# Weights stored by column tiles, squares of x by columns, a conv unit in spare banks and late gate parts by quadrant, in a one-layer hybrid decoder step

## The reference

```python
q, k, v, h, B, C = split(rms_norm(x) @ w_in)            # 6 x 1024 columns
a = dilated_attention(q_normed, k_normed, v)            # 16 heads of 64
c = B * short_conv(C * h)
h1 = x + concat[rms_norm(a), rms_norm(c)] @ w_out
h2 = h1 + (silu(n @ w_gate) * (n @ w_up)) @ w_down      # n = rms_norm(h1), D_FF 5632
y = h2 + sigmoid(rms_norm(h2) @ w_ple_gate) * (p @ w_ple_proj)
```

## Time and profile before

| | |
|---|---|
| median of 3 runs | 2556.58 us (2554.0 to 2557.53) |
| the profiled execution's own time | 2558.73 us |
| its span, first to last instruction | 2557.2 us |
| TensorE busy | 2487.2 us (97%), 20452 matmuls |
| VectorE, ScalarE, GpSimd busy | 1744.7 (68%), 934.6 (37%), 254.2 (10%) us |
| mean granted TensorE clock | 0.989 of 2.4 GHz (its other level is 0.5, 1.2 GHz) |
| DMA | 328.26 MB, 128 GB/s in the mean |

### The profile page before, as it was taken

One profiled execution on the slowest core, in us unless ns is written; L12 is line 12 of the kernel. 1 busy time (PEld: TensorE's weight loads), 2 busy tenths in 40 slices (PEclk: granted clock), 3 DMA queues, 4 the chain that ended last, 5 costly groups with the idle time before them and its releaser, 6 DMA issues.

```text
span 2557.2 us, 51857 instructions
## 1 busy us (share of the span) xinstructions
PE 2487.2 (97%) x20452; PEld 2470.9 (97%) x20452; DVE 1744.7 (68%) x2185; ACT 934.6 (37%) x1202; POOL 254.2 (10%) x285
## 2 busy tenths in 40 slices
PE   5999999999999989999999999999999999999998
PEld 5999999999989979999999999999899999999998
DVE  3576877787786879888888898898533322356433
ACT  4232333333332444444444444444332211233331
POOL 1111110111021000000000000000000000143000
PEclk8999999999999989999999999999999999999999
DMA  7444343434334434544444454444665543233342
GB/s 230 134 127 121 107 123 95 120 109 126 107 110 135 133 91 117 152 127 133 132 115 136 127 148 131 116 132 117 207 212 171 164 145 121 83 92 99 110 116 66
DMA packets 477677, 328.26 MB, mean 128 GB/s; under 512 B 18330, under 2 KB 452762, under 8 KB 476584
## 3 DMA queue, kind: packets, MB, share of 16 engines
q1 hardware_dynamic: 449488, 250.25, 34.6%
q0 software_dynamic: 27248, 74.89, 8.9%
q10 hardware_dynamic: 880, 2.31, 0.3%
HBM read 291.06 MB, written 40.65 MB: 130 GB/s over the span
## 4 chain that ended last, share of the span: by engine, by line
PE 89%; DMA 4%; DVE 4%; issue 1%; ACT 1%; POOL 0%; DVEq 0%; SPq 0%; ACTq 0%
PE acc L538 17%; PE acc L542 17%; PE acc L540 16%; PE acc L731 11%; PE acc L730 11%; PE acc L732 11%; DMA wraw<-in_w_in 3%; DMA wraw<-in_w_down 1%; DVE wlo L1172 1%; PE aux L549 1%; PE aux L581 1%; ACT whi L845 0%; PE aux L625 0%; DVE slots_c L1180 0%; PE aux L554 0%
## 5 line engine op out<-in xcount | busy, mean ns | idle before, releaser
L1172 DVE TENSOR_TENSOR wlo<-wraw,whi 128x1024 fp32r<-128x1024 f32 (+1 forms) x276 | 333.1, 1207 | 421.2 <-ACT whi L845 420.5
L845 ACT ACTIVATE whi<-wraw 128x1024 fp32r<-128x1024 f32 (+1 forms) x276 | 285.3, 1034 | 729.8 <-PE acc L542 616.5
L730 PE MATMUL acc<-xb_hi,whi 128*128 128x260 f32 x1232 | 349.4, 284 | 11.9 <-DVE xb_lo L1553 11.9
L731 PE MATMUL acc<-xb_lo,whi 128*128 128x260 f32 x1232 | 349.6, 284 | 0.0
L732 PE MATMUL acc<-xb_hi,wlo 128*128 128x260 f32 x1232 | 349.1, 283 | 0.0
L730 PE MATMUL acc<-xa_hi,whi 128*128 128x260 f32 x1232 | 348.8, 283 | 0.0
L732 PE MATMUL acc<-xa_hi,wlo 128*128 128x260 f32 x1232 | 348.8, 283 | 0.0
L731 PE MATMUL acc<-xa_lo,whi 128*128 128x260 f32 x1232 | 348.7, 283 | 0.0
L538 PE MATMUL acc<-slots_a,whi 128*128 128x260 f32 x1536 | 314.9, 287 | 0.0
L542 PE MATMUL acc<-slots_a,wlo 128*128 128x260 f32 x1536 | 310.2, 284 | 0.0
L540 PE MATMUL acc<-slots_a,whi 128*128 128x260 f32 x1536 | 308.3, 282 | 0.0
(11 more groups left out here) (266 smaller groups left out, 4980.4 us busy)
## 6 DMA issues: line engine op xcount, KB each, us to landing
wraw<-in_w_in SPq DMA_DIRECT2D x96, 512.0 KB, 4.0
blocks<-in_w_gate SPq DMA_DIRECT2D x88, 512.0 KB, 6.3
blocks<-in_w_up SPq DMA_DIRECT2D x88, 512.0 KB, 6.1
wraw<-in_w_down SPq DMA_DIRECT2D x48, 448.0 KB, 3.7
wraw<-in_w_out SPq DMA_DIRECT2D x32, 512.0 KB, 3.9
wraw<-in_w_ple_gate SPq DMA_DIRECT2D x32, 512.0 KB, 3.9
slots_b<-f_dram SPq DMA_DIRECT2D x28, 520.0 KB, 4.7
f_dram<-sig_t POOLq DMA_DIRECT2D x22, 520.0 KB, 3.2
```

The source lines that it names most:

```text
L730: mm(to, w_h, hi[:, n, X_OF[u], :], start=p == 0, stop=False)
L731: mm(to, w_h, lo[:, n, X_OF[u], :], start=False, stop=False)
L845: on(whi[:, u % HILO, 0:width], wraw[:, u % RAW, 0:width], ACT.Copy).then_inc(s_whi, 1)
L1172: V.tensor_tensor(wlo[:, u % HILO, 0:width], wraw[:, u % RAW, 0:width], whi[:, u % HILO, 0:width].bitcast(F32), ALU.subtract).then_inc(s_w ...
```

## The change

- **Weights by column tiles.** On the host every weight matrix is laid out as [column tile, 128 partitions, k tiles x 128], so that a unit is one run of 4 KB for each partition where it was eight of 512 B. Which bytes are loaded when is the same. The gate and up blocks keep even and odd k tiles apart.
- **The start.** The first weight goes ahead of x on SP's queue, and x's first load moves to ACT's. The second copy of x by rows is gone, with POOL's four loads and its wait for them; the keys' load follows the skew and row-bias stores at once. ScalarE squares the 16 column tiles (5, 5 and 6 of them behind the splits of weights 4, 5 and 6), VectorE adds them up, and TensorE sums the result by columns behind unit 2. The root and the reciprocal come in the same places of the lists as before.
- **The conv half.** The root goes ahead of ScalarE's split of weight 4, and the queries' upper halves one step later. VectorE's reciprocal comes first; its split of weight 4 and `norm_q` follow the first output tile. The transposes go to the scores' bank, and unit 2 to the two spare banks of the attention, so it waits for neither accumulator.
- **The gate's start.** The parts' upper and lower halves are made by kind (all even tops, all odd halves, then the sums). The sums of pair 6 get buffers of their own, and are added beside the attention half; the fourth sum has its sign turned when it is added, with negated gains. TensorE begins with the first four units on the early parts (the third in spare banks), then finishes unit 0 on the even tops, most of unit 2 on the odd ones, and units 1 and 3 as the sums come. The last square and the norm's sum come behind unit 4.

```diff
+X_SQUARES = (range(0, 5), range(5, 10), range(10, KT))
...
-            sp.dma_start(wraw[:, u % RAW, 0:nk * width].rearrange("p (k m) -> p k m", k=nk),
-                         w[k0 * P:(k0 + nk) * P, bass.ds(col, width)].rearrange("(k p) m -> p k m", p=P)
-                         ).then_inc(landed[u % RAW], 16)
+            sp.dma_start(wraw[:, u % RAW, 0:nk * width],
+                         w[bass.ds(tile, 1), :, k0 * width:(k0 + nk) * width].squeeze(0)).then_inc(landed[u % RAW], 16)
...
                 if first and n == 0:
-                    load_x(2)
-                load(at, 2 * n + 1, w_in, KU, KU, j * P + kind)
+                    load_x(1)
+                    load_x(3)
+                load(at, 2 * n + 1, w_in, KU, KU, j + kind // P)
                 if first and n == 0:
-                    load_x(4)
-                    load_x(6)
-
-        load_x(0)
+                    load_x(5)
+                    load_x(7)
...
+                if a is None and g == 2:
+                    pe.wait_ge(s_bias, 1)
+                    pe.wait_ge(s_xadd, KT - 1)
+                    column_sums(x_sum).then_inc(s_nsum, 1)
...
         pe.wait_ge(s_ninv, N_CONV)
-        pe.wait_ge(s_o, 2 * (KA - 1))
+        pe.wait_ge(s_biased, 8 * (KA - 1))
         for b in range(QB):
-            nc.tensor.transpose(aux[:, BANK_O, b * P:(b + 1) * P], gsq[:, b:b + 1].broadcast_to([P, P]), ident[:, :])
+            nc.tensor.transpose(aux[:, BANK_S, b * P:(b + 1) * P], gsq[:, b:b + 1].broadcast_to([P, P]), ident[:, :])
...
         for i in range(2, KT):
-            pe.wait_ge(s_read, T_CONV + i - 1)
-            unit(at, i, mixed, range(KC), i % 2, True, True)
+            if i == 2:
+                pe.wait_ge(s_v2, KA)
+                pe.wait_ge(s_o, 2 * (KA - 1))
+                unit(at, i, mixed, range(KC), None, True, True, to=spare)
+                pe.wait_ge(s_wide, 2)
+            else:
+                pe.wait_ge(s_read, T_CONV + i - 1)
+                unit(at, i, mixed, range(KC), i % 2, True, True)
+            if i == 3:
+                pe.wait_ge(s_read, T_CONV + 3)
             if 2 <= i <= PAIR_UNITS + 1:
                 attention(KA - 1, i - 2, final=True)
...
+        def first_products(at):
+            for u in range(4):
+                pe.wait_ge(s_wlo, at.count(u))
...
+                for p in range(EARLY):
+                    pe.wait_ge(s_xp, p + 1)
+                    triple(first_to(u), u, u, p)
+            for p in range(EARLY, KP2):
+                pe.wait_ge(s_lo_a, p - EARLY + 1)
+                done = triple(first_to(0), 0, 0, p)
+            done.then_inc(s_unit, 1)
+            for p in range(EARLY, KP2 - 1):
+                pe.wait_ge(s_lo_b, p - EARLY + 1)
+                triple(first_to(2), 2, 2, p)
+            for p in range(EARLY, KP2):
+                pe.wait_ge(s_xp, p + 1)
+                done = triple(first_to(1), 1, 1, p)
+                if p == KP2 - 1:
+                    done.then_inc(s_unit, 1)
+                    triple(first_to(2), 2, 2, p).then_inc(s_unit, 1)
+                done = triple(first_to(3), 3, 3, p)
+            done.then_inc(s_unit, 1)
...
+        def square_x(t):
+            if t > 2:
+                act.wait_ge(s_xadd, t - 2)
+            on(x_sum if t == 0 else tmp[:, t % 2, :], hid[:, t, :], ACT.Square).then_inc(s_xsq, 1)
...
+            if a is None and g < 3:
+                for t in X_SQUARES[g]:
+                    if t > 0:
+                        dve.wait_ge(s_xsq, t + 1)
+                        if t > 1:
+                            dve.wait_ge(s_xadd, t - 1)
+                        V.tensor_tensor(x_sum, x_sum, tmp[:, t % 2, :], ALU.add).then_inc(s_xadd, 1)
...
             dve.wait_ge(s_read, T_CONV + i + 1)
             dve.wait_ge(l_res[i % 2], 16 * (i // 2 + 1))
             V.tensor_tensor(hid[:, m, :], act_t[:, :], res[:, i % 2, :], ALU.add).then_inc(s_h, 1)
+            if i == 0:
+                split(at, HILO)
+                norm_q(KA - 1, KA - 2)
             if i == 1:
                 q_lo(KA - 1)
...
+        for p in range(EARLY, KP2):
+            dve.wait_ge(s_hi_a, p - EARLY + 1)
+            even_top_lo(p).then_inc(s_lo_a, 1)
+        for p in range(EARLY, KP2):
+            dve.wait_ge(s_hi_b, p - EARLY + 1)
+            odd_lo(p).then_inc(s_lo_b, 1)
+        dve.wait_ge(d_h[1], 16)
+        sums_lo(EARLY)
+        sums_lo(EARLY + 1)
+        parts_added(KP2 - 1)
+        blocks_ahead(Span(U_G), 0, 0, HILO)
+        dve.wait_ge(d_h[2], 16)
+        dve.wait_ge(s_lo_b, EARLY)
+        sums_lo(EARLY + 2)
+        sums_lo(EARLY + 3)
+        square_added(KT - 2)
         square_added(KT - 1)
...
-        for g in range(PIECES):
-            pool.wait_ge(l_x[g], 16)
-        for b in range(QB):
-            pool.dma_start(x_nat[:, b, :], x_prompt[0, b * P:(b + 1) * P, :]).then_inc(l_xn[b], 16)
-        pool.wait_ge(s_xsq, QB + 1)
         load_keys(0)
...
+    def columns(name, width=P, parts=1):
+        w = given[name][0]
+        w = w.reshape(w.shape[0] // (parts * P), parts, P, w.shape[1] // width, width)
+        return np.ascontiguousarray(w.transpose(3, 2, 1, 0, 4).reshape(w.shape[3], P, -1))
```

More of the change, by code:

```diff
@@ L271, in build, with halves, sums_of, sum_groups @@
     t_odd = tmp[:, 0:2, :].rearrange("p a t -> p (a t)").rearrange("p (n h) -> p n h", h=HALF)
-    parts = (t_even, t_odd)
+    def halves(tile):
+        return tile.rearrange("p (h t) -> p h t", h=2)
+    third = (halves(acc_attn), halves(rstd[:, :]))
+    def sums_of(p):
+        if p == KP2 - 2:
+            return [third[0][:, 0, :], third[0][:, 1, :], third[1][:, 0, :], third[1][:, 1, :]]
+        return [(t_odd if p % 2 and p < KP2 - 1 else t_even)[:, n, :] for n in range(4)]
+    def sum_groups(p):
+        if p == KP2 - 2:
+            return [(3, 5, third[0]), (5, 7, third[1])]
+        return [(3, 7, (t_odd if p % 2 and p < KP2 - 1 else t_even)[:, :, :])]
     q1_t, v2_t, v3_t, v25_t = (t_even[:, n, :] for n in range(4))
@@ L521, in _, with unit @@
         mm = nc.tensor.matmul
-        def unit(at, u, operand, tiles, slot, first, last, ready=None, between=None, n0=0, signal=True):
+        def unit(at, u, operand, tiles, slot, first, last, ready=None, between=None, n0=0, signal=True, to=None):
             pe.wait_ge(s_wlo, at.count(u))
+            to = acc_of(slot) if to is None else to
             for n, kt in enumerate(tiles):
@@ L550, in spread_sum, with column_sums @@
             return done
+        def column_sums(tile):
+            for b in range(QB):
+                mm(aux[:, BANK_D, b:b + 1], tile[:, b * P:(b + 1) * P], ones[:, 0:1], start=True, stop=True)
+            return mm(aux[0:DEC, BANK_D, QB:QB + 1], tile[:, SEQ:T], ones[:, 0:1], start=True, stop=True)
         def products(out, hi, lo, rhi, rlo, begin, end):
@@ L759, in gate_up @@
                     pe.wait_ge(s_ev, it * 24 + (6 * r + 2))
-                begun = first and u in (0, 1, 3)
-                done = triples(w, u, range(EARLY if begun else 0, KP2), ready=begun)
-                done.then_inc(s_unit, 1)
-                if first and u == 1:
+                triples(w, u, range(KP2)).then_inc(s_unit, 1)
+                if first and u == 4:
                     pe.wait_ge(s_hsum, KT - 1)
@@ L1083, in gate_up @@
                     split(Span(U_D), w + HILO - 7 * TURN, DOWN[0][0] * P)
-                if first and u == 2:
+                if first and u == 4:
                     act.wait_ge(s_nsum, N_FFN)
@@ L1552, in parts_lo @@
-            V.tensor_tensor(lo[:, n, 3:6, :], parts[p % 2][:, 0:3, :], hi[:, n, 3:6, :].bitcast(F32), ALU.subtract)
-            V.scalar_tensor_tensor(lo[:, n, 6, :], parts[p % 2][:, 3, :], -1.0, hi[:, n, 6, :].bitcast(F32),
-                                   ALU.mult, ALU.subtract).then_inc(s_xp, 1)
+            for first, last, source in sum_groups(p):
+                done = V.tensor_tensor(part_lo(p, first, last), source, part_hi(p, first, last).bitcast(F32), ALU.subtract)
+            done.then_inc(s_xp, 1)
```

300 lines of the change are left out of this document (159 added, 141 removed).

## The result

The changed kernel takes **2536.24 us** (median of four runs, 2534.33 to 2538.43), the kernel before 2555.82 on the same chip: a ratio of 0.9921, 95% interval 0.9907 to 0.9935. The forecast was 2533.9 in a range of 2523 to 2548. The profiled execution took 2535.68 us (span 2534.1), against 2558.73 (2557.2) before: 23.05 us by the two profiles, 3.5 more than by the medians (19.6), since the execution profiled before lay 2.9 above its median.

The account below looks back on a forecast made before the run. TensorE bounds the kernel, never idle in full flow; the change can reach only its 81 us of losses. Gains 5.3 + 7.5 + 0 + 8.5 + 3.5 = 24.8 against 2558.73 give 2533.9 us, range 2523 to 2548.

Parts of the forecast that it names:

- the sum of 24.8: Whole kernel: gains in us of start 5.3, first attention pair 7.5, conv half 0, gate 8.5, first down units 3.5.
- the sum of turns: Weight loads beside POOL: engines take one packet of each queue in turn, so 1.9 + 8 x 0.33 = 4.5 us.
- Rival B: Weight loads beside POOL: turns go by bytes, so weights land no sooner; 2553.1 us, chance 0.12.
- the 1 us for eight of POOL's turns: Argument against B's skill-page support: with 9 to 17 pieces per turn, POOL would delay a small load only 1 us.
- it lands at 29.7: Start: weight 4, issued at 25.2 us, lands at 29.7; the splits and adds then end at 46.1.
- the 11.6 that I gave: Start: the first unit begins at 11.6 us, after x at 6.6, table load, x upper halves and weight halves.
- units 3 to 5 are queued behind: Start: after the third unit TensorE's column sums need all 15 adds, with these units behind; TensorE idles 15 us.
- a bound of 8.1: First attention pair, 116 to 216 us: upper bound of the 7.5 us gain, equal to the loss there before.
- Rival E: Conv half: the queries' parts come in time for the third unit; 7 us more gain, 2526.9 us, chance 0.09.
- Rival D: Gate: its list stays bound by VectorE and TensorE meets the same pauses later; gain 0 there, 2542.4 us, chance 0.10.
- then 8 x 0.33 = 2.6: First down units: a 256 KB load beside POOL falls from 32 x 0.165 = 5.3 us to 2.6.
- Rival C: Start: column sums park TensorE, coming at 73 us instead of 46; slower, 2571.7 us, chance 0.05.

## Why the prediction was right, and where not

The mechanisms of the layout, of the first pair and of the gate came as forecast; that the sum of 24.8 came near the 23.0 of the traces (19.6 by the medians) is in part luck. The start (3.3 too high), the first down units (0.8) and the pace of the matmuls (1.1, a term put at nothing) were made up for by the first pair and the gate, 1.4 too low each, and by 0.6 elsewhere.

**Weights by column tiles: right in kind, too high in size.** 4 KB runs shorten loads beside POOL, and the runs of 512 B and 1 KB show that it is the runs. But the sum of turns gave 4.5 us for a load, and 6.5 to 7.6 were measured, outside the 4 to 6 that were to show it right: an engine doesn't simply take one packet of each queue in turn, nor are all engines alike (last section). Between 512 B and 4 KB the packets fell to an eighth, the time over the quiet load only from 9 or 10 us to some 3 or 4. Rival B (turns by bytes, loads as late as before) is out. One step against it was wrong: the 1 us for eight of POOL's turns prices each at one piece, while eight turns for SP's 64 pieces give SP eight to a turn. With eight pieces to POOL's turn as well it is 8 x 8 x 0.134 = 8.6 us (an estimate from the earlier trace rows), so 13.21 beside 3.91 doesn't contradict such turns.

**Start: 5.3 forecast, 2.0 measured.** The step that failed is "it lands at 29.7": the fifth weight was issued at 25.84 (25.2) and landed at 32.3, 2.0 late in itself. With 0.6 from the issue and 0.7 from the steps behind it the sums came at 49.4 instead of 46.1, and these 3.3 us are the whole miss in this execution; in the three others with the same start the sums came at 49.7 to 50.6. The first unit also began 2.5 us after the 11.6 that I gave: x's first load took 7.68 us, and I had priced it as if it were alone behind the weight; it goes out with seven other x loads, the second weight and the tables, but that their company is the cause isn't shown. That cost nothing, as the sums decide. The pause of 15.03, which was forecast at 15, is right only because both its ends moved.

What the prediction never did is to price the parts of the start apart: the column tiles give 7.9 us there and the rest of the start takes 5.8 back, most of it by the sums' place in TensorE's list (4.8 by the kernel that only moves them). It said that "units 3 to 5 are queued behind" the sums, which is the cost, and stopped at netting it.

**First attention pair: 7.5 forecast, 8.9 measured.** Full, as forecast. The stretch of 116 to 216 holds 70 matmuls more than in the earlier trace rows, which is 8.4 us at 0.1196 us each; the pause that went began a little ahead of it. I had taken 7.5 of a bound of 8.1 without a row for the difference.

**Conv half: 0 forecast, 0.1 measured**, by the steps as they stand: the pause ahead of the scores is 6.67 us (6.5 forecast) and ends on the queries' lower halves; undoing the edit changes nothing that can be told. Rival E is out.

**Gate: 8.5 forecast, 9.9 measured, 9.8 by the kernel without the edit.** VectorE's list came as worked out: four top parts in 1.68 us, four odd ones in 2.77, one pause of 4.23 ahead of the last parts (5 forecast). The half clock that goes with it lasted 6.8 us, from 918.0 to 924.8, in place of the 17 before. Rival D is out.

**First down units: 3.5 forecast, 1.9 measured at that point, and 1.4 with the column tiles alone.** The step that failed is "then 8 x 0.33 = 2.6" for a load that had taken 5.3; in the chain of waits of the changed kernel the two loads are

```profile
1798.29 7.40 DMA wraw<-in_w_down
...
1817.91 9.35 DMA wraw<-in_w_down
```

against 7.82 and 10.85 in the earlier trace rows, so they fell by 0.4 and 1.5 us. They share SP's queue with eight loads of hidden tiles of 520 KB, and the DMA engines are busy for 84% of that stretch before and after. The last pause went from 3.0 to 1.7 us. The other 0.8 of the 2.7 after that point is the matmuls' pace, below.

Rival C was right about its place, not about its size: the sums do park TensorE with three units behind, but at 49 us, not 73.

## What to carry to other kernels

Small runs cost little while a queue is alone and double a load's time beside another queue's traffic; so read the landing of a load where another queue is busy, not the mean. Before a reduction is moved onto a busy in-order engine, look at which ready units stand behind it: here one place in TensorE's list was worth 5 us, and work put where VectorE idled anyway, with one read moved ahead of it, another 13.6. When a wait is taken away, read who releases the next one; four times here it was an accumulator's read that stood behind other work in VectorE's list (v's twice, the second and the third conv unit's once each).

## What the runs showed that I had not expected

**DMA engines that are not full still hold a load up.** While the changed kernel's load of 66.9 us was out (6.9 us, against 3.3 quiet), both queues together took 40% of the 16 engines' time. The DMA view of 66 to 75 us: packets, MB, share.

```profile
q1 hardware_dynamic: 148, 0.54, 20.7%
q0 software_dynamic: 1738, 0.34, 19.5%
```

So the mean share doesn't say when a load lands. The packet records of the traces say what it waits for: two of the sixteen engines. Each load ends with 16 packets of 4 B, one for each engine as I read them. Of this load's, 14 were sent by 71.7 us and the other two at 72.6 and 73.5. With runs of 512 B the load issued at 73.6 us, which landed at 88.0, has 14 by 78.4 and the other two at 87.3 and 87.6; SP's row of the DMA view of that kernel, from 73.6 to 78.5 and from 78.5 to 80.2 us, where this load is the only one out:

```profile
q1 hardware_dynamic: 917, 0.46, 34.2%
```

```profile
q1 hardware_dynamic: 18, 0.01, 1.8%
```

With the queues quiet, all 16 of a 4 KB load lie within 0.3 us (102.9 to 103.1). So in these two loads the last two engines set the landing, and with small runs they are 9 us behind the other fourteen; why two are slow beside POOL's stores, no run here settles.

**The pace of matmuls in full flow depends on the program.** Windows of 1000 to 1780 us and 1900 to 2280 us, both at clock 1.00 with no pause: first the kernel before, then the changed one.

```profile
1000.00:1780.00 780.00, 780.00 (x6496) 780.00 (x6496) 696.28 (x754) 345.36 (x388) 57.51 (x77) 1.00 0.47 131
1900.00:2280.00 380.00, 380.00 (x3168) 380.00 (x3167) 143.34 (x140) 87.57 (x86) 35.51 (x31) 1.00 0.42 132
```

```profile
1000.00:1780.00 780.00, 780.00 (x6487) 780.00 (x6487) 694.25 (x752) 345.54 (x387) 58.34 (x79) 1.00 0.39 132
1900.00:2280.00 380.00, 380.00 (x3172) 380.00 (x3172) 146.01 (x140) 91.26 (x90) 42.53 (x33) 1.00 0.42 129
```

Nine matmuls fewer in the gate's flow (1.1 us) and four more in the down stage (0.5 us). All nine experiments that keep the gate's edit have 119.87 ns per matmul in the second window and 120.28 in the first, the two without it 120.05 and 120.12 like the kernel before; the loops issue the same matmuls in both. It goes with the gate's edit, not with the weights' layout. That edit also splits a buffer in two and adds another, which may move operands in on-chip memory; whether that is the cause was not tried.
